# A two-block transformer on one core: the entry of the even layer's attention steps reordered, GpSimd's weight splits halved

## The reference

```python
def even_mixer(h, w_in, cmp_pe, cmp_w1, cmp_w2, w_out, cos, sin):
    proj = jnp.einsum('btd,de->bte', h, w_in)
    qa, ka, va, qi, ki, wi, qb, kvb, gb = split_cols(proj, EVEN_SPLITS)
    # rotary positions on qa, ka, qi, ki, qb, k_c, k_s, k_w
    o_a = dsa_attention(qa, ka, va, qi, ki, wi)
    o_b = nsa_attention(qb, k_c, v_c, k_s, v_s, k_w, v_w, gb, cmp_pe, cmp_w1, cmp_w2)
    return jnp.einsum('bte,ed->btd', jnp.concatenate([o_a, o_b], -1), w_out)
```

## Time and profile before

| what | us |
|---|---|
| median of three runs | 1945.93 |
| range of the runs | 1945.81 to 1953.98 |
| the profiled execution | 1947.74 |
| its span in the trace | 1945.9 |
| TensorE busy | 1857.2 (95%) |
| VectorE busy | 965.8 (50%) |
| ScalarE busy | 796.5 (41%) |
| GpSimd busy | 472.4 (24%) |

### The profile page before, as it was taken

How to read it: one execution, slowest core, us unless ns; L and a number is a source line. 1 busy time by engine, 2 the same in 40 slices (tenths; PEclk the granted TensorE clock), 3 DMA queues, 4 the chain that set the end, 5 groups by cost and what they waited for, 6 DMA issues and landing times.

```text
span 1945.9 us, 24560 instructions
## 1 busy us (share of the span) xinstructions
PE 1857.2 (95%) x9678; PEld 1461.6 (75%) x9682; DVE 965.8 (50%) x1571; ACT 796.5 (41%) x1401; POOL 472.4 (24%) x471
## 2 busy tenths in 40 slices
PE   6999998999999989999999999999999899999997
PEld 5987776766677756667888888877887688888885
DVE  5355554574546677744533333354566454333334
ACT  4235663445435355554442313233444344232322
POOL 0025551101313124541120201004666212010200
PEclk9999999999999979999999999999999899999998
DMA  4321111221013310001223223222121022222231
GB/s 152 98 76 49 51 44 55 76 87 33 22 55 95 125 44 23 23 23 49 93 97 98 94 90 103 92 87 65 55 66 55 22 98 98 99 97 98 91 101 68
DMA packets 40289, 143.32 MB, mean 74 GB/s; under 512 B 4592, under 2 KB 4976, under 8 KB 40176
## 3 DMA queue, kind: packets, MB, share of 16 engines
q1 hardware_dynamic: 40176, 141.76, 22.4%
HBM read 139.64 MB, written 2.10 MB: 73 GB/s over the span
## 4 chain that ended last, share of the span: by engine, by line
PE 87%; DVE 5%; ACT 3%; POOL 3%; issue 1%; DMA 1%; DVEq 0%; SPq 0%; POOLq 0%; ACTq 0%
PE BANK L275 22%; PE BANK L277 22%; PE BANK L276 22%; PE BANK L856 2%; PE BANK L629 2%; PE BANK L1626 2%; PE BANK L1583 1%; PE BANK L1607 1%; PE BANK L2394 1%; PE BANK L913 1%; DVE LH L719 1%; PE BANK L2369 1%; PE BANK L614 1%; PE BANK L2356 1%; PE BANK L2357 1%
## 5 line engine op out<-in xcount | busy, mean ns | idle before, releaser
L252 ACT ACTIVATE WH<-WRAW 128x1024 fp32r<-128x1024 f32 x262 | 273.5, 1045 | 494.7 <-PE BANK L277 460.8
L261 DVE TENSOR_TENSOR WL<-WRAW,WH 128x1024 fp32r<-128x1024 f32 (+1 forms) x249 | 324.8, 1305 | 259.8 <-ACT WH L252 259.6
L275 PE MATMUL BANK<-HH,WH 128*128 128x512 f32 x1048 | 426.9, 407 | 20.4 <-DVE WL L261 18.2
L277 PE MATMUL BANK<-HL,WH 128*128 128x512 f32 x1048 | 410.4, 392 | 0.0
L276 PE MATMUL BANK<-HH,WL 128*128 128x512 f32 x1048 | 410.2, 391 | 0.0
L275 PEld LDWEIGHTS BANK<-HH,WH 128*128 128x128 f32 x1048 | 198.0, 189 | 70.6 <-ACT WH L252 18.9
L276 PEld LDWEIGHTS BANK<-HH,WL 128*128 128x128 f32 x1048 | 198.2, 189 | 43.1 <-issue 5.3
L277 PEld LDWEIGHTS BANK<-HL,WH 128*128 128x128 f32 x1048 | 197.8, 189 | 42.8
L2253 POOL TENSOR_TENSOR HID<-TMP,HID 128x512 fp32r<-128x512 f32 x64 | 83.0, 1297 | 528.4 <-ACT HID L2234 528.4
L277 PE MATMUL BANK<-HID,WH 128*128 128x512 f32 x512 | 202.3, 395 | 0.0
L275 PE MATMUL BANK<-HID,WH 128*128 128x512 f32 x512 | 202.2, 395 | 0.0
(11 more groups left out here) (388 smaller groups left out, 3159.7 us busy)
## 6 DMA issues: line engine op xcount, KB each, us to landing
WRAW<-in_w SPq DMA_DIRECT2D x77, 512.0 KB, 3.4
WRAW<-in_wu SPq DMA_DIRECT2D x64, 512.0 KB, 3.2
WRAW<-in_wd SPq DMA_DIRECT2D x64, 512.0 KB, 3.2
WRAW<-in_w0o SPq DMA_DIRECT2D x8, 512.0 KB, 3.5
WRAW<-in_w1o SPq DMA_DIRECT2D x8, 512.0 KB, 3.5
WRAW<-in_wc SPq DMA_DIRECT2D x8, 512.0 KB, 3.2
WRAW<-in_w2o SPq DMA_DIRECT2D x8, 512.0 KB, 3.3
WRAW<-in_w3o SPq DMA_DIRECT2D x8, 512.0 KB, 3.4
```

Of the source, the lines that this page charges most:

```text
L252: e.activation(WH[b % NS][:, 0:n], WRAW[b % NR][:, 0:n], ACT.Copy).then_inc(*inc("s_high", ("high", b)))
L261: e.tensor_tensor(WL[b % NS][:, 0:n], WRAW[b % NR][:, 0:n], WH[b % NS][:, 0:n].bitcast(F32), ALU.subtract).then_inc(*inc("s_low_pool" if p ...
L275: e.matmul(dst, ah, bh, start=first and i == 0, stop=False)
L277: made = e.matmul(dst, ah, bl, start=False, stop=last and i == len(sets) - 1)
```

## The change

Six edits, all in the even layer.

- ScalarE makes the second gelu, the sigmoid and both table loads before the window keys. `keys` is cut in two; the four swaps (`swapped`) of the window keys come behind the high half of the first queries.
- VectorE turns the window keys and the first queries before it splits any weight, and takes query tile 8 before it splits tile 9's weights. The splits of tiles 10 and 11 go to steps 4 and 5.
- TensorE makes `second(1)` inside tile 8 and turns the c values before the loop. It turns tile 8 in step 1, while VectorE and GpSimd take that turned tile in step 3. The fills start in step 1, with one empty step more at 22, so tiles 9 to 11 end a step earlier and 12 to 14 where they ended.
- The third index sum goes from step 1 to step 2, behind the second maximum, the c values' copies from step 2 to 3.
- No selection round is made in steps 0 to 2.
- GpSimd makes a block's low half in two instructions of 512 columns, two and three steps after the step in which the tile ended, not in one in that step.

```diff
+        def split_low_half(e, w, b, half):
+            n = stream[b][2] // 2
+            c = slice(n * half, n * half + n)
+            w.wait_ge(*at("used", b - NS))
+            w.wait_ge(*at("high", b))
+            e.tensor_tensor(WL[b % NS][:, c], WRAW[b % NR][:, c], WH[b % NS][:, c].bitcast(F32),
+                            ALU.subtract).then_inc(*inc("s_low_pool", ("low", b) if half else ("low half", b)))
...
-        E_FILL0, E_FILL = 2, (1, 2, 1, 1, 2, 1, 0)
+        E_FILL, E_REST = (1, 2, 1, 1, 2, 1, 0), 22
+        def e_place(step):
+            return step - 1 - (step >= E_REST)
...
-            return E_Q + 1 if step == 1 else e_ended(step - 1)
+            return E_Q + 1 if step == 3 else e_ended(step - 1)
...
# TensorE
                 if k == 2:
                     rot_of(E_Q)
-            second(1)
+                if k == 4:
+                    second(1)
+            c_values()
...
-                if e_turning(step) is not None:
+                if step == 1:
+                    rot_of(E_Q + 1)
+                elif step > 3 and e_turning(step) is not None:
                     rot_of(e_turning(step), (7,))
-                if step == 2:
-                    c_values()
...
# VectorE
             taken(E_Q)
+            after_rope(E_KW)
+            after_rope(E_Q)
+            keys(1)
+            c_keys(1)
+            taken(E_Q + 1)
             split("e", E_Q)
-            after_rope(E_KW)
-            keys(1)
-            after_rope(E_Q)
-            taken(E_Q + 1)
-            split("e", E_Q + 1)
-            c_keys(1)
-            split("wc2", 1)
...
-                if step == 1:
+                if step == 2:
                     index_sum(3)
-                if step == 2:
+                if step == 3:
                     c_values()
+                if step == 4:
+                    split("e", E_Q + 1)
+                if step == 5:
+                    split("wc2", 1)
...
-                for _ in range(1 if busy or step % 2 else 2):
+                for _ in range(0 if step < 3 else 1 if busy or step % 2 else 2):
...
# ScalarE
             split("e", E_Q)
-            keys(1)
-            high(E_Q)
             gelu(1)
             e.activation(gates, gates, ACT.Sigmoid).then_inc(*inc("s_gates", ("gates",)))
             e.preload_act_table_set("natural_log_exp_and_others")
+            keys(1)
+            high(E_Q)
+            swapped(1)
...
# GpSimd
+            gelu_low(1)
             cos(E_Q)
-            gelu_low(1)
...
-                if e_ended(step) is not None:
-                    split("e", e_ended(step))
+                for half in range(2):
+                    if e_ended(step - 2 - half) is not None:
+                        split_low_half(e, w, block["e", e_ended(step - 2 - half)] + NS, half)
```

11 lines of the change are left out of this document (5 added, 6 removed).

## The result

The changed kernel took 1940.48 us (median of 15 runs, 1934.28 to 1943.99) against 1948.42 (15 runs, 1945.16 to 1953.98) for the kernel before beside it: ratio 0.9956, 95% interval 0.9944 to 0.9968. The forecast, 11.5 us or 0.59% less, lies outside both intervals; the gain is 0.3 to 0.44%, under the 0.5% that the prediction took as its bound, so of its three outcomes the one at 0.42, no change, came, and not the one at 0.55. The time of 1940.48 lies outside the forecast's own range, 1931 to 1938, and inside the wide one, 1929 to 1941.5. The kernel before, too, was 2.5 us slower beside it (1948.42) than the 1945.93 to which the forecast was set.

The account below looks back on a forecast made before the run. TensorE, busy for 95% of the span, was taken to bound the kernel by its work, waits and clock. Terms of 6 + 4.0 + 2.3 - 0.8 = 11.5 us off gave 1934.5 us; own range 1931 to 1938, 8-in-10 range 1929 to 1941.5.

Parts of the forecast that it names:

- three outcomes: Whole kernel against a 0.5% bound: faster (under 1936.2 us) 0.55, no change 0.42, slower (over 1955.7 us) 0.03.
- Term 1: Entry of the step loop: early gelu and late weight splits bring `scores(4)` forward; 6 us gained, bounds 3.5 and 9.
- Term 2: GpSimd's splits as later halves: its waiting for ScalarE's weight copy goes; 4.0 us gained, bounds 9.4 and -6.
- 0.5 for each of six tiles: GpSimd's halves: cost in us added for a half following `low` in front of the next scale, 3.0 in all.
- rival A: Half the gain: entry clock stays low, loop makes as many waits as it removes bar 2; 1940 us, chance 0.27.
- E: Slower: in every tile's steps a half precedes a scale TensorE wants, and the clock falls; 1953 us, chance 0.04.
- Term 3: Clock in the loop: falls to 0.50 behind waits at 759.27 and 811.52 go; 2.3 us gained, bounds 0 and 3.1.
- no 0.50 window after 725: Sign for the loop's clock: no window with 0.50 granted after 725 us.
- Term 4: Selection rounds moved out of steps 0 to 2 land in steps 32 to 34: -0.8 us, between 0 and -3.
- port rule: VectorE and GpSimd share an exclusively locked port pair; a half holds VectorE up no longer than the half's length.
- Rival C: VectorE's adds finishing a query's turn are held by halves, 1.27 us once per tile, six times; 1940.6 us, chance 0.06.

Follow-up runs that it names:

- f4: Changed kernel with second gelu, sigmoid and table loads put back behind the window keys and first queries; ratio 0.9964 to the kernel before, stage 209.96 us.
- g1: Kernel before with only VectorE's two weight splits (tiles 10 and 11) moved to steps 4 and 5; ratio 0.9975 to the kernel before, stage 213.42 us.
- g2: Changed kernel with the four selection rounds kept in steps 0 to 2; ratio 0.9997 to the kernel before, stage 212.95 us.
- f3: Changed kernel with GpSimd's twelve split halves cut to 8 of 512 columns each; ratio 0.9949 to the kernel before, stage 207.70 us.
- g3: Changed kernel, tile 11's weight copy behind step 2's exponentials, last tile's halves one step later, tile 11's two; 1933.72 us, ratio 0.9930 to before.
- f2: Changed kernel with GpSimd's two halves of the last tile's split one step later; ratio 0.9958 to the kernel before, stage 207.99 us.
- e2: Changed kernel with GpSimd's splits whole and back in their old step; ratio 1.0004 to the kernel before, stage 210.73 us.

## Why the prediction was right and wrong

- **Term 1, the entry: right in kind, too small.** Forecast 6 (3.5 to 9), measured 8.5 within the stage. The chain weight split, load, copy, `exps(0)` came as written, 1.2 us earlier: 3.6 us from issue to copy, not 4.3. Another 1.2 is the clock: the prediction had it back 5.7 us after `scores(2)` as before; it was back 4.5 us after, at 709, having been at 0.50 for 3.4 us only, and from `scores(2)` to `scores(4)` it took 6.3 us, not 7.5. The forecast's 6 also counted the moved eighth (0.7), which the 8.5 does not; counted alike the entry is 9.2, past its bound of 9. In the windows of the entry TensorE's idle time fell by 3.6 us (7.9 to 4.3) and its busy time by 4.9.
- **Its causes were ordered wrongly.** The text began with gelu and tables; they are worth 0.6 (f4). VectorE's splits alone give 2.0 at the second unit, 2.55 of the stage (g1). The absent rounds give about 1.9 at the entry (g2). Those three don't add up to 8.5: f4 and g2 take one edit away with the others in place, g1 adds one alone. That each only uncovers the next in VectorE's queue fits g1's rows; the index sum's own share was not run.
- **Term 2, GpSimd's splits: the step failed.** Forecast 4.0 gained; 9.4 us of waits became 9.4 (7.4 + 2.0). The wait of GpSimd for ScalarE's copies went, as forecast, but f3 shows that 6.3 us are there without any split, where I left 1.3. The "0.5 for each of six tiles" was in truth 1.1 at each of two tiles and nearly nothing at the others. The wait left at VectorE's row of five small instructions was 1.98, not 1.1. The 1.5 us for ScalarE's copies had no term at all. This was rival A's and E's mechanism at two of six places: a half in front of a scale that TensorE wants. At the last tile no eighth covered it; at 780.89 the one eighth of the step (778.33) was not enough.
- **Term 3, the clock in the loop: failed with it.** Forecast 2.3; two stretches of 3.4 us before (760, 811; the prediction read 3.1), two after (804, 862). The "no 0.50 window after 725" of the prediction is refuted. g3 reached it. That each stretch costs half its length held at 862 (f2: 2.8 us with the wait's 1.2) and not at 804, which cost nothing.
- **Term 4, the rounds: right as far as it went.** I priced the late rounds at -0.8, and late they cost about 1 us, in the forecast steps (g2). But I gave their absence at the entry no term of its own, where four rounds would have cost about 1.9. As a whole the edit gained.
- **The sum.** 8.5 - 1.9 = 6.6 stands against 11.5: an entry 2.5 too small and a loop 7.4 too good (4.0 + 2.3 - 0.8 = 5.5 expected, -1.9 found). The errors partly cancelled, and that 1940.48 still fell into the wide range owes something to this. Rival A had the loop ("as many waits as it removes bar 2") and the time, 1940, but for the entry the wrong reason: it kept the clock low there.
- **The port rule** (the Trainium skill, "SBUF — State Buffer", "SBUF: two separate sides") did not decide. Rival C's adds (L1760) took 0.67 or 0.68 us at every tile of the changed kernel, so no half held one up. (In e2 two took 0.97 and 1.19, beside scales of GpSimd, not beside a split.) And f3, with no half of any length, gains 2.5 us at most, nearly all of it at the two waits named above. What VectorE did lose beside GpSimd was at another instruction: an instruction of 8 elements (L1853) took 1.21 us at 801.16, beside GpSimd's cosine (801.08, 1.26 us), just ahead of L1856, for which TensorE waited 1.98; elsewhere it takes about 0.2. f3 has the same row, so the splits have no part in it.

What stays open: why e2's runs are slower than its profile, and what sets whether the clock falls behind a given wait.

## What to carry to other kernels

Where an engine waits ahead of the critical instruction, list everything behind that wait in its queue and price the whole row: here a removed wait of 4.6 us was worth 2 to 2.5, and four selection rounds of 0.9 us behind it another 1.9. Before a piece of work is put "where there is slack", look at each repetition: at four of six tiles a half cost nothing, at two it cost 1.1 us each, and at one of these 1.6 more by the clock. A claim that moved work costs nothing is read at the place where it went, not from the stage's total: g2's total hid 1 us for the late rounds. A stage whose gain shows mostly as clock should be followed unit by unit in two profiles, since one profile's total can be off by as much as the change is worth.
